# Hybrid decoder step on one Trainium2 core: where and when the paged sample loads are issued

## The reference, cut to what matters

```python
PAST_LEN, PAGE_SIZE = 2048, 128          # 16 pages for each of the 8 samples
sel_s = gather_blocks_paged(cache_kv_slc, page_table, kv_slc_s, idx_s)   # selected blocks
o_slc_s = slc_attend(q_rot_s, sel_s, idx_s, valid_s, pos_s)
o_win_s, win_s = win_sample(q_rot_s, kv_win_s, cache_kv_win, pos_s)      # last 512 rows
o_mem_s = mem_attend(mq_raw, cache_kv_mem, mem_q_norm)                   # 256 memory rows
```

## Time and profile before

| what | us |
|---|---|
| median of three executions | 2466.98 |
| the profiled execution's own time | 2464.73 |
| its span | 2463.1 |
| PE busy in the span | 2299.4 |
| POOL busy | 285.3 |
| the two sample blocks, from start to end | about 1037.7 to 1172.8 |

### The profile page before, as it was taken

One profiled execution on the slowest core, in us unless ns is written; L12 is line 12 of the kernel. 1 busy time (PEld: TensorE's weight loads), 2 busy tenths in 40 slices (PEclk: granted clock), 3 DMA queues, 4 the chain that ended last, 5 costly groups with the idle time before them and its releaser, 6 DMA issues. The chain is left out here.

```text
span 2463.1 us, 39913 instructions
## 1 busy us (share of the span) xinstructions
PE 2299.4 (93%) x15431; PEld 2130.6 (86%) x15431; DVE 1154.1 (47%) x2060; ACT 802.2 (33%) x1795; POOL 285.3 (12%) x549
## 2 busy tenths in 40 slices
PE   6998798999877999857999999999999999999999
PEld 6977798999766899834899999878999999999997
DVE  4547766312758877634422233335333443333335
ACT  5355364444345666423312122213211111111110
POOL 1004221003203422244000000000000000000000
PEclk9999699999998999988999999999999999999999
DMA  5011442321110000176112132211111111111111
GB/s 155 27 35 44 144 129 86 109 103 35 45 37 1 1 2 18 48 235 211 42 49 52 39 86 52 86 48 52 52 52 52 35 52 52 35 52 52 35 35 69
DMA packets 177129, 156.73 MB, mean 64 GB/s; under 512 B 24770, under 2 KB 158069, under 8 KB 176884
## 3 DMA queue, kind: packets, MB, share of 16 engines
q1 hardware_dynamic: 158660, 120.37, 16.7%
q0 software_dynamic: 7136, 19.07, 2.6%
q10 hardware_dynamic: 11152, 14.80, 1.8%
HBM read 142.76 MB, written 15.59 MB: 64 GB/s over the span
## 5 line engine op out<-in xcount | busy, mean ns | idle before, releaser
L181 PE MATMUL ps<-brT_r,ff_wih 128*128 128x344 f32 x1008 | 322.4, 320 | 0.0
L183 PE MATMUL ps<-brT_r,ff_wi_r 128*128 128x344 f32 x1008 | 322.0, 319 | 0.0
L182 PE MATMUL ps<-xnT_r,ff_wih 128*128 128x344 f32 x1008 | 321.8, 319 | 0.0
L3935 ACT ACTIVATE ff_sa<-ps 128x344 f32<-128x344 f32 x66 | 30.2, 458 | 563.5 <-PE ps L183 563.5
L181 PEld LDWEIGHTS ps<-brT_r,ff_wih 128*128 128x128 f32 x1008 | 189.9, 188 | 1.0
L183 PEld LDWEIGHTS ps<-brT_r,ff_wi_r 128*128 128x128 f32 x1008 | 189.7, 188 | 0.0
L181 PE MATMUL ps<-x_r,mg_wh 128*128 128x344 f32 x576 | 185.2, 321 | 4.7 <-DVE xnT_r L169 4.7
L182 PEld LDWEIGHTS ps<-xnT_r,ff_wih 128*128 128x128 f32 x1008 | 189.1, 188 | 0.4
L182 PE MATMUL ps<-xnT_r,mg_wh 128*128 128x344 f32 x576 | 184.5, 320 | 0.0
L3971 DVE TENSOR_TENSOR x<-x,ps 128x512 f32<-128x512 f32 (+1 forms) x198 | 134.9, 686 | 100.9 <-PE ps L183 100.1
L183 PE MATMUL ps<-x_r,mg_w_r 128*128 128x344 f32 x552 | 176.4, 320 | 0.0
(11 more groups left out here) (667 smaller groups left out, 5625.7 us busy)
## 6 DMA issues: line engine op xcount, KB each, us to landing
ff_wi<-in_w_ffn_in SPq DMA_DIRECT2D x42, 512.0 KB, 5.1
mg_w<-in_w_in SPq DMA_DIRECT2D x23, 512.0 KB, 4.1
ff_wo<-in_w_ffn_out SPq DMA_DIRECT2D x11, 1024.0 KB, 4.9
s_pages<-in_cache_kv_slc SPq DMA_DIRECT2D x64, 128.0 KB, 4.7
s_pages<-in_cache_kv_slc POOLq DMA_DIRECT2D x64, 128.0 KB, 3.1
sc_X<-in_cache_kv_cmp SPq DMA_DIRECT2D x56, 128.0 KB
sc_X<-in_cache_kv_cmp POOLq DMA_DIRECT2D x56, 128.0 KB, 2.4
mg_w<-in_w_branch SPq DMA_DIRECT2D x23, 256.0 KB, 4.5
```

Of the source, the lines that this page charges most:

```text
L181: nc.tensor.matmul(out, wh, xh, start=(first and k == 0), stop=False)
L182: nc.tensor.matmul(out, wh, xl, start=False, stop=False)
L183: ins = nc.tensor.matmul(out, wl, xh, start=False, stop=(last and k == n - 1))
L3935: nc.scalar.activation(sa[:, s % 2, :], ps[:, s % 2, 0:BLK], ACT.Silu).then_inc(silued, 1)
```

## The change

The first row of the page table is also loaded into a free stretch of `x2` during the prompt's attention, and sample 0's pages are issued with it at the start of `stage_s_select`, on POOL ahead of the mask. Sample 1's pages move from `stage_s_select` to `stage_s_attend`: on SP to its start, on POOL behind the key copies of sample 0. The window and memory rows of samples 2 to 7 move from ACT's queue to SP's, each ahead of SP's page loads for the same sample and behind a wait for `attended_w`.

```diff
--- before.py
+++ after.py
@@ -211,7 +211,7 @@
         M["spilled"], M["tok_in"], M["tok_in1"], M["tok_high"] = (
             nc.alloc_semaphore(n) for n in ("spilled", "tok_in", "tok_in1", "tok_high"))
         M["mg_in"] = [nc.alloc_semaphore(f"mg_in{i}") for i in range(2)]
-        M["n_out"] = nc.alloc_semaphore("n_out")
+        M["n_out"], M["pt_in"] = nc.alloc_semaphore("n_out"), nc.alloc_semaphore("pt_in")
         M["kc_kept"] = nc.dram_tensor("kc_kept", (HD, B * G * NCS), F32, kind="Internal").ap()
         M["vc_kept"] = nc.dram_tensor("vc_kept", (P, B * G * HD), F32, kind="Internal").ap()
         M["gS"] = top.enter_context(nc.sbuf_tensor("gS", [B, 280], F32))[:, :]
@@ -1876,7 +1876,7 @@
 
 
 
-    nc, ps, c, brT = (M[k] for k in ("nc", "ps", "c", "brT"))
+    nc, I, ps, c, brT = (M[k] for k in ("nc", "I", "ps", "c", "brT"))
     qr, gk, kvsw, kT, acc = (A[k] for k in ("qr", "gk", "kvsw", "kT", "acc"))
     units = [(i, h, br) for i in range(QT) for h in range(H) for br in range(2)]
 
@@ -1963,6 +1963,7 @@
             @block.sync
             def _(sp):
 
+                sp.dma_start(first_pages(M), I["page_table"][0:1, :]).then_inc(M["pt_in"], 16)
                 sp.wait_ge(pturned, last_q + 1)
                 for dst, name in zip(kept_rows(M), ("kc_kept", "vc_kept")):
                     sp.dma_start(dst, M[name]).then_inc(M["kept_in"], 16)
@@ -2408,6 +2409,12 @@
         page = eng.value_load(pt[0:1, bass.ds(n * 2 + (half + NPG * b), 1)], min_val=0, max_val=NPHYS - 1)
         eng.dma_start(dst[:, bass.ds(n * 512 + half * 256, 256)],
                       cache[bass.ds(page, 1)].rearrange("o r g c d -> r (o g c d)")).then_inc(done, 16)
+
+
+def first_pages(M):
+
+
+    return M["x2"][:, :, :].rearrange("p t d -> p (t d)")[0:1, 8704:8704 + NPG].bitcast(I32)
 
 
 def load_kv(eng, cache, pages, pt, b, half, done, free=None):
@@ -2790,13 +2797,14 @@
             def _(sp):
 
                 sp.dma_start(A["pt"][:, :], I["page_table"].rearrange("b n -> (b n)").unsqueeze(0)).then_inc(A["pt_in"], 16)
-                sp.wait_ge(A["pt_in"], 16)
-                for b in range(2):
-                    load_kv(sp, I["cache_kv_slc"], A["pages"], A["pt"], b, 0, A["in_p"][0])
+                sp.wait_ge(M["pt_in"], 16)
+                load_kv(sp, I["cache_kv_slc"], A["pages"], first_pages(M), 0, 0, A["in_p"][0])
 
             @block.gpsimd
             def _(pool):
                 nc.gpsimd.memset(tri[:, :, :], 1.0).then_inc(tri_ok, 1)
+                pool.wait_ge(M["pt_in"], 16)
+                load_kv(pool, I["cache_kv_slc"], A["pages"], first_pages(M), 0, 1, A["in_p"][1])
                 pool.wait_ge(tri_ok, 1)
 
                 for j in range(4):
@@ -2804,11 +2812,8 @@
                     nc.gpsimd.affine_select(out=mine_, in_=mine_, compare_op=ALU.is_ge, fill=0.0, base=NJ * j - 1,
                                             pattern=[[1, NJ], [-1, NB]], channel_multiplier=0).then_inc(tri_ok, 1)
                     pool.wait_ge(tri_ok, j + 2)
-                pool.wait_ge(A["pt_in"], 16)
-                load_kv(pool, I["cache_kv_slc"], A["pages"], A["pt"], 0, 1, A["in_p"][1])
                 pool.wait_ge(scored, 1)
                 compact_win_keys(nc.gpsimd, A["rows"][0], kw, 0, A["in_win"], A["kcomp"])
-                load_kv(pool, I["cache_kv_slc"], A["pages"], A["pt"], 1, 1, A["in_p"][1])
 
             @block.tensor
             def _(pe):
@@ -3030,13 +3035,20 @@
         with st.block() as block:
             @block.sync
             def _(sp):
+                sp.wait_ge(A["pt_in"], 16)
+                load_kv(sp, I["cache_kv_slc"], pages, pt, 1, 0, in_p[0])
                 for b in range(2, B):
+                    sp.wait_ge(attended_w, b - 1)
+                    load_win(sp, I["cache_kv_win"], rows[b % 2], b, in_win[b % 2])
+                    load_mem(sp, I["cache_kv_mem"], rows[b % 2], b, in_mem[b % 2])
                     load_kv(sp, I["cache_kv_slc"], pages, pt, b, 0, in_p[0], (attended_s, b - 1))
                 load_merge_first(M, sp)
 
             @block.gpsimd
             def _(pool):
                 compact_page_keys(pool, pages, ks, 0, in_p, kcomp)
+                pool.wait_ge(A["pt_in"], 16)
+                load_kv(pool, I["cache_kv_slc"], pages, pt, 1, 1, in_p[1])
                 for b in range(1, B):
                     if b > 1:
                         pool.wait_ge(turned, FILLS * (b - 1) + 1 - DONE)
@@ -3227,10 +3239,6 @@
 
                 for b in range(B):
                     f = FILLS * b
-                    if 1 <= b < B - 1:
-                        act.wait_ge(attended_w, b)
-                        load_win(act, I["cache_kv_win"], rows[(b + 1) % 2], b + 1, in_win[(b + 1) % 2])
-                        load_mem(act, I["cache_kv_mem"], rows[(b + 1) % 2], b + 1, in_mem[(b + 1) % 2])
                     for n in range(f if b else DONE, f + 5):
                         if n % 2 == 0:
                             keep(act, n)
```

## The result

| what | before | after |
|---|---|---|
| median of nine executions each, us | 2466.42 | 2473.35 |
| lowest to highest, us | 2463.50 to 2467.99 | 2468.41 to 2477.98 |
| profiled execution's own time, us | 2464.73 | 2475.3 |
| sample blocks, start to SP's closing drain, us | 135.2 | 142.9 |

The ratio is 1.0027 with an interval of 1.0016 to 1.0037: slower by 0.27%, just over what was to be called no change, and 2.05 us above the range. The forecast was wrong. Of the cases listed, the second rival (2473.2 us) comes nearest.

The account below looks back on a forecast made before the run. Bounds: the gap between sample blocks, 9 us loading a sample not yet needed, and POOL's loop of 9.73 us plus tail. 8.5 - 1.9 - 5.1 + 0.4 = 1.9 us gained, median 2465.1 us, range 2457.0 to 2471.3.

Parts of the forecast that it names:

- second rival: POOL's turn grows more: six page DMAs of every turn meet rows, tail 5.4 us each, 2473.2 us in all; chance 0.12.
- L: Tail of POOL's turn, from its last page issue to the next first key copy; taken as 4.2 us with rows.
- c(0): Start of POOL's first page key copy of sample 0; forecast 8.5 us earlier, at 1054.9 instead of 1063.38.
- c(0) to c(2): First key copy of sample 0 to that of sample 2: two whole POOL turns, 27.56 us against 25.66, 1.9 lost.
- c(2) to c(6): First key copy of sample 2 to that of sample 6: four turns of 13.93, 55.7 us against 50.65, 5.1 lost.
- c(6) to c(7): First key copies of samples 6 and 7: merge loads some 2 us earlier against POOL's pages, 0.4 us gained.
- c(7) to the end: From sample 7's first key copy to the end of the second block: nothing left to load, 0 us.
- merge part: Sample 7's turn: merge loads stand earlier against POOL's pages, tail 5.0 for 5.4 us, 0.4 gained, bounds 0 and 1.5.
- Half clock: Where PE's clock is lower, `attended_w` comes 8.8 us after the sample's first key copy, making the tail 4.0 us.
- first rival: The rows cost POOL's pages little: tail 2.6 us gives 2455.8 us, 3.1 gives 2458.8; chance 0.36 of over 4.9 gained.
- The third: First block shrinks less: POOL's drain might last until all loads are in, 2467 us; counted under no change, no separate chance.
- In by about 1053: At the first block's end, the 5 MB of loads need 14.5 us from 1037.7 and would not hold the barrier.

## Why the prediction was wrong

**The step that failed is the size of L beside the rows.** The prediction took 4.2 for a turn with rows in it, from a line between 4.3 (a POOL page DMA issued with the rows) and 5.4 (an SP page DMA issued 1.8 behind them), which gave "1.2 behind: 5.0". The second point was of another engine's queue. A POOL page DMA 0.7 us behind the memory rows (1.2 behind the window rows) is waited for until 7.9 to 9.1 us after its start, and its tail is 7.3 to 8.5. Over the six turns the tail was 6.0 on average where the sum had 4.2 (3.9 for sample 1). Part by part, for the two profiled executions:

| part | forecast, us | measured, us |
|---|---|---|
| c(0) | -8.5 | 17.7 - 25.7 = -8.0 |
| c(0) to c(2) | +1.9 | 31.5 - 25.7 = +5.8 |
| c(2) to c(6) | +5.1 | 63.8 - 50.7 = +13.1 |
| c(6) to c(7) | -0.4 | 11.8 - 15.2 = -3.4 |
| c(7) to the end | 0 | +0.1 |
| stage | -1.9 | +7.7 |

Of the 9.6 us between the two sums, c(0) to c(6) makes some 12, and the merge part takes 3 back. The tails of c(0) to c(2) were 4.2 and 7.6 for 3.9 and 4.2: 3.7 us. Those of c(2) to c(6) sum to 24.3 for 16.8: 7.5 us. The remaining 0.7 or so are turns that took 9.85 on average and not 9.73 outside the tail.

**Half clock.** It was put in as a mere discount (L = 4.0 where `attended_w` comes later). The event was right, c + 9.35 for the forecast's c + 8.8, but it feeds back: a late `attended_w` makes a short tail, this gives the clock back, and the next tail is long (read from the trace, as above). A mean L hid that.

**The rivals.** The second gave 2473.2 us and has the mechanism (page DMAs slowed by rows) and the sign; its price was 5.4 in each turn, and the mean of the six is (4.2 + 7.6 + 4.2 + 8.0 + 3.7 + 8.5) / 6 = 6.0. That it names nearly the measured median is partly luck: the sample turns cost 4.2 us more than it said and the merge part gave 3.4 back. What was argued against it, that only the last three DMAs of a turn meet the rows, is true and does not help: the copy waits for the last one. The first rival is out. The Trainium skill's page "DMA: Bandwidth & Descriptors" (Queues, rings and completion order) says that a DMA engine takes turns between queues, and the prediction worked out a tail of 3.1 from equal turns; the long tails of 7.6 to 8.5 disagree with that working. The third is out too: POOL's drain ended at 1055.3 and the barrier was open at 1055.6, while page data of sample 0 still landed at 1056.7, so the drain does not last until all loads are in.

**What held.** The block end (forecast 17.0 behind the start, measured 16.6); the mask at no cost; SP's later page half hidden (for sample 3 its issues end at 1084.43 + 4.71 = 1089.1, and POOL's begin at 1093.3). For c(0) the end of the chain moved: the copy waits 5.11 us for pages after POOL's last work. SP's last page DMA of sample 0 started at 1048.0 and took 8.7 us, to 1056.7, while the barrier was open at 1055.6. "In by about 1053" was thus 3.7 us out for an execution that starts 1.4 us later. It cost 0.5 us of the 8.5. Whether the rows of sample 1, which share the queues then, are what holds it was not tried.

**The merge part** gained 3.4 for 0.4: SP issues the merge loads at 1152.59, and POOL's first page DMA of sample 7 follows only at 1157.12. They were out of the way, and the last tail was 2.1. SP had run that far ahead because the turn had grown: that is read from the issue times, and no run tried it in this kernel.

Summed in the waits view of POOL from 1031 to 1192 us (engine, tile, line, what it waited for: total us, times, longest), after and then before:

```profile
POOL s_rows L2459 <- DMA s_pages<-in_cache_kv_slc: 39.0, 8, 7.9
```

```profile
POOL s_rows L2452 <- DMA s_pages<-in_cache_kv_slc: 21.0, 6, 7.5
```

18 us more are spent waiting for pages, against 9 us taken from the block end: but for 1 us, that difference is the stage's 7.7.

**What stays open.** Why POOL's pages move so slowly beside the rows, while SP's later ones do not. The trace shows how the engines' time went. In the DMA view of the changed kernel from 1081 to 1087 us, q1 is SP's queue and q0 POOL's (packets, MB, share of 16 engines):

```profile
DMA packets 1124, 2.11 MB, mean 352 GB/s; under 512 B 104, under 2 KB 780, under 8 KB 1123
...
q1 hardware_dynamic: 978, 1.70, 78.7%
q0 software_dynamic: 145, 0.39, 18.9%
```

The 0.39 MB are POOL's last three page DMAs, the 384 KB of the first rival. By equal turns they would have taken some 2.2 us (an estimate, from half of the 352 GB/s); they took all six. It is not that packets are unlike: the trace has POOL's pages and the memory rows in packets of 4 KB both, the window rows in 1 KB. From 1086.2 on only four packets of q0 are left, one of them with data. So POOL's pages do not wait for the rows' end at 1088.6; they get a fifth of the engines while the rows are on their way. With the rows on ACT's queue the share is the same (0.39 MB against 1.52 in the six us from 1110). What sets it was not taken apart: no run split the rows into smaller DMAs, or put pages on a queue other than SP's or POOL's.

## What to carry to other kernels

Space that is free is not yet the moment to load into it. Before a large transfer is released earlier, ask which small DMA ends the current wait and when that one is issued, and tie the large one to that issue (here one wait on a count that exists). Where an engine reads registers for its DMAs, put the reads where it would wait anyway: here that got the small DMAs ahead of the large one and made the fastest kernel. And when one value stands for a quantity in every turn, look whether a late and an early turn feed each other.

## What the runs showed of the hardware

A 128 KB page DMA of POOL takes 2.4 us in the quiet part of its turn. When it is issued 0.7 us behind a 1 MB load of memory rows, on SP's queue or on ACT's, the copy that waits for it starts only 7.9 to 9.1 us after its own start, about when the 1 MB is in (1088.2 against 1088.6; in another kernel 1145.7 against 1145.3). Meanwhile POOL's queue moved 0.39 MB in 6 us beside 1.70 MB on SP's. SP's page DMAs issued 5 us behind the same load took 2.6.

A register read on POOL and a DMA issue on POOL add up, to 1.13 us a pair, while four reads ahead of the copies brought POOL's first DMA from c + 5.1 to c + 2.9.

PE's granted clock was 1.00 before and 0.50 after a stretch of 5.5 us without work, and window attention then ended 1.4 us later (c + 9.35 for c + 7.98), enough to decide which of two transfers was issued first.
